# Opening of a two-block transformer kernel: the first modulation computed with its weights stationary, and the first norms and products taken in blocks of features

## Chip, cores and metric

The kernel runs on one core of a Trainium2 chip. The metric is the device time of one execution in microseconds, the median over several executions. Matrix products run on TensorE (PE; its weight loads are listed as PEld), element work on VectorE (DVE), ScalarE (ACT) and GpSimd (POOL); SyncE (SP) issues most transfers.

## What is computed

Two transformer blocks over 256 tokens of width 1024, in fp32. The opening of the first block is what the change touches:

```
c_act = silu(c); c_ctx_act = silu(c_ctx)
shift, scale = (c_act @ w_ada[:, 0:2048] + b_ada[0:2048]) split in two     # for x, and the same for ctx
h     = rmsnorm(x,   g_mix) * (1 + scale)   + shift                        # latent stream
h_ctx = rmsnorm(ctx, g_mix) * (1 + scale_c) + shift_c                      # context stream
dd, k, v = h @ w_in[:, ...]   and the same three from h_ctx
log_a = log_sigmoid(dd @ w_dec_up + b_dec) / 16                            # decays of the linear attention
```

After it come a chunked gated linear attention in both directions, a convolution branch, a merge, a gated feed-forward net, and the second block (feed-forward, two attentions, feed-forward). The factors of modulation are 1024 x 2048 numbers of `w_ada` (8 MB) applied to two vectors only, `c` and `c_ctx`.

## The kernel before, in words

**Precision.** A product of activations and weights is made of three fp32r products, hi*hi, hi*lo, lo*hi. `split` (ACT: L840, DVE: L1833) makes the two parts of a 1 MB weight unit: ACT copies `raw` to `whi`, DVE subtracts to get `wlo`. The units stand in a ring of three. Plain fp32 products (`mm` on fp32 tiles) are recorded as two matmuls each. Every matmul has a weight load of its own.

**Units.** The first block is a list `P1` of units of 256 columns of `w_in`: dd (decay factors), k0, k1, v0 to v3, q0, q1 and so on. Units dd, k and v are made for both streams, latent (tiles A) and context (tiles B). Each engine has its program in a fixed order written by hand; semaphores tie them. For unit `u`, ACT and DVE evacuate unit `u-1`, split unit `u+2`, and then do their part of the attention (`gla_front`, `gla_step`).

**The opening.** SP issues the loads in this order: the three vectors c, two 1 MB blocks of `w_ada`, eleven small vectors, two blocks, ctx, x, four blocks, the units. PE takes `w_ada` as the moving operand: for each of 8 blocks 8 products with a stationary [128, 2] (c and c_ctx), moving 256 columns (L1756 and the loop before it), into rows [2, 512] of four banks. ACT brings the rows to `arow`, PE turns them into columns by 16 small transposes (L1756), DVE adds biases and gain (`columns`, L1853). `norm(n)` on PE (L1323) transposes the normalised ctx (n = 0) and x (n = 1), 16 transposes each; `modulate` (ACT, L882) and `affine`, `low` (DVE, L1881, L1886) apply the factors and split into hi and lo parts. All of `w_ada` has to be multiplied before any factor is used. Then PE makes unit dd by `first_product`, k0 half 0, `gla(U_K, 0)`, that is `decay_products(0)` and `(1)` (16 recorded matmuls over 32 rows, L1371), k0 half 1, and unit k1 with `decay_products(2)`, `(3)` in its middle.

**The decay chain.** From the decay products on, ACT (`log_decays`, `soft_part`, `decays`, L972 to L992) and DVE (`log_decays`, `sums`, `decayed_keys`, L2017 to L2074) work through absolute value, exp, log, prefix sums and exp again. The split of unit 4 (v1) stands on DVE behind the sums of the first pair of passes, that of unit 5 (v2) behind the sums of the second pair. `turn_keys` (L1387) transposes the decayed keys in the middle of v2 and v3.

**GpSimd** forms the inverse roots of the norms, builds constants, and then computes the later modulation blocks (`adapt`, L750 to L759), each behind a 1 MB load of its own; the first of these loads waits for the end of the factors (`as_mm`), the first `adapt` for all hi and lo parts (`hlo_done` 16).

**Later norms.** `shift_and_scale` (L1357), before norms 2 to 5, makes its columns in the other way: stationary a [128, 128] fp32 piece, moving one column of ones, 16 products, recorded as 32.

Of the kernel before, what the change touches and what calls it, by code (L numbers as in the profile page):

```python
# [15 lines left out]
P = 128  # L16
D = 1024
T = 256
# [40 lines left out]
def unit_banks(base, plan):  # L59

    banks, held, before = [], {}, []
    for n, (kind, m) in enumerate(plan):
        if n == 0:
            b = [0, 7] if kind == "dd" else [0]
# [82 lines left out]
def build(nc, a, out):  # L147
    with ExitStack() as ctx:
# [72 lines left out]
        arow = ada_raw[0:2, :, :].rearrange("p a b -> p (a b)")  # L221
# [31 lines left out]

        XN = at3(24, TT, D)
        HF = at3(32, KD, T)
        HF1 = [at3(0, KD, T), at3(8, KD, T)]
# [63 lines left out]
        ada0_mm = sem("ada0_mm")  # L320
        ada0_row = sem("ada0_row")
# [145 lines left out]
        def unit_source(kind, n):  # L467
# [7 lines left out]
            if kind in first:  # L475
                w, c0 = first[kind]
                return cview(w, c0 + UC * n), KD, UC
# [20 lines left out]
        def _(sp):  # L498
# [54 lines left out]
            for j in range(8):  # L553
                if j == 2:

                    for name, r0 in VEC.items():
                        v = a[name]
                        n = math.prod(v.shape) // P
                        src = bass.AP(tensor=v.tensor, offset=0, ap=[[P, n], [1, P]])
                        sp.dma_start(vrows[r0:r0 + n, :], src).then_inc(vec_in, 16)  # L560
                    for name, r0, n in (("b_ada", 0, 48), ("b_ada_2", 48, 72)):
                        src = bass.AP(tensor=a[name].tensor, offset=0, ap=[[P, n], [1, P]])
                        sp.dma_start(brows[r0:r0 + n, :], src).then_inc(vec_in, 16)
                sp.dma_start(ada0[j], a["w_ada"][0].rearrange("(p k) n -> p k n", k=KD)[:, :, UC * j:UC * j + UC])\  # L564
                    .then_inc(start_ada[j], 16)
                if j == 3:
                    sp.dma_start(ctxX, a["ctx"].rearrange(tok, p=P)).then_inc(x_in[0], 16)
                    sp.dma_start(X[:], a["x"].rearrange(tok, p=P)).then_inc(x_in[1], 16)

            for u, (kind, n) in enumerate(P1):  # L570
                load_unit(u, kind, n)
# [34 lines left out]

        def norm_dest(n):
            return (B_hi, B_lo) if n == 0 else (A_hi, A_lo)

        def norm_bank(n, b):  # L610

            return {0: (4, 5, 6, 0), 1: (1, 2, 3, 4), 2: (5, 6, 7, 2), 5: (4, 6, 7, 2)}.get(n, (4, 5, 6, 2))[b]
# [20 lines left out]

        def norm_fp32(n):
            return HF1[n] if n < 2 else HF

# [36 lines left out]
        def _(pool):  # L673
# [93 lines left out]
            norm(0)  # L767
            norm(1)
# [19 lines left out]
            for d in range(2):  # L788
                pool.dma_start(wdec[RANK * d:RANK * d + RANK, d, :], a["w_dec_up"][0, d]).then_inc(dec_in, 16)
            load_ada(0)  # L790
# [38 lines left out]
        def _(act):  # L829
# [52 lines left out]
            def modulate(n):  # L882
                s = 1 if n == 0 else 0
                h, (hi, lo) = norm_fp32(n), norm_dest(n)
                act.wait_ge(as_done, max(1, n))

                def affine(k, o):
                    return run(o[:, k, :], bank[norm_bank(n, k // 2)][:, k % 2 * T:k % 2 * T + T], ACT.Identity,
                               bias=shift[:, s, k:k + 1], scale=scale[:, s, k:k + 1])

                def high(b):
                    if n == 1:
                        act.wait_ge(h_dve, b + 1)
                    else:
                        act.wait_ge(h_done, b + 1)
                    run(hi[:, 2 * b:2 * b + 2, :], h[:, 2 * b:2 * b + 2, :]).then_inc(hhi_done, 1)

                if n == 1:
                    for b in range(4):
                        high(b)  # L900
                    return
                if n == 0:
                    for b in range(4):
                        act.wait_ge(tr_done, b + 1)
                        for k in (2 * b, 2 * b + 1):
                            ins = affine(k, h)
# [1584 lines left out]
```

## Time and profile before

| | us |
|---|---|
| median of 3 runs | 1217.5 |
| lowest, highest | 1215.88, 1219.05 |
| the profiled execution | 1218.4 |
| its span, first to last instruction | 1216.6 |
| PE busy | 1166.5 (96%) |
| DVE busy | 853.4 (70%) |
| ACT busy | 574.0 (47%) |
| POOL busy | 325.1 (27%) |
| mean granted clock of TensorE | 0.976 |

The span is the time from the first to the last instruction of that one execution; its own time is 1.8 us longer. Busy PE time counts matmuls from start to modelled end, so it says nothing of how fast they follow each other: for that, divide the length of a row of the timeline by its count.
### The profile page before, as it was taken

The numbers are of one execution on the slowest core, as the hardware profiler recorded it, in microseconds if no ns is written. First come the engines' busy times: TensorE is split into PE (matmuls) and PEld (weight loads), VectorE is DVE, ScalarE is ACT, GpSimd is POOL, SyncE is SP. The second block draws the span as 40 slices with busy tenths as digits, with TensorE's granted clock in tenths as the row PEclk, the third lists the DMA queues.
The fourth block names the chain that finished last, engine by engine and source line by source line (L and its number), as shares of the span: only waits on it lengthen the run. The fifth ranks groups of instructions, "written<-read, shape, count | busy, mean of one in ns | idle before, by whom it ended". The sixth has DMA issues, their size and how long they took to land.

```text
span 1216.6 us, 18692 instructions
## 1 busy us (share of the span) xinstructions
PE 1166.5 (96%) x7600; PEld 1040.7 (86%) x7600; DVE 853.4 (70%) x935; ACT 574.0 (47%) x734; POOL 325.1 (27%) x219
## 2 busy tenths in 40 slices
PE   6899999999999899999989999999999989999996
PEld 2599988999999888888878888889998989888885
DVE  0478474489577778877778877788766587755676
ACT  1566434354443364444555444445654625544452
POOL 1376573066565200000020000011156663000000
PEclk9899999999999899999989999999999989999999
DMA  9643645365866648777747777755954655656670
GB/s 310 218 139 105 208 144 168 105 217 186 273 232 218 203 169 275 242 254 257 267 147 255 254 252 246 261 161 190 298 181 149 201 186 179 204 177 201 213 258 35
DMA packets 192354, 250.59 MB, mean 206 GB/s; under 512 B 4763, under 2 KB 171870, under 8 KB 192158
## 3 DMA queue, kind: packets, MB, share of 16 engines
q1 hardware_dynamic: 183838, 217.44, 54.9%
q0 software_dynamic: 8448, 32.18, 7.7%
q8 instruction: 50, 0.82, 0.3%
q14 instruction: 18, 0.15, 0.0%
HBM read 248.56 MB, written 1.05 MB: 205 GB/s over the span
## 4 chain that ended last, share of the span: by engine, by line
PE 77%; DVE 13%; ACT 4%; issue 3%; SPq 2%; DMA 1%; POOL 0%; POOLq 0%; DVEq 0%; ACTq 0%
PE twin L1272 74%; DVE arena L1819 4%; DVE wlo L1819 3%; ACT arena L838 2%; DVE arena L1827 2%; SPq L564 1%; DMA raw<-in_w_in 1%; ACT whi L838 1%; PE twin L1340 1%; DVE X L1819 1%; DVE A_both L1819 1%; PE twin L1607 0%; DVE B_lo L1819 0%; DVE X L1827 0%; ACT L838 0%
## 5 line engine op out<-in xcount | busy, mean ns | idle before, releaser
L1272 PE MATMUL twin<-A_both,whi 128*128 128x256 f32 (+1 forms) x2224 | 584.7, 340 | 2.5 <-DVE arena L1819 1.1
L1819 DVE TENSOR_TENSOR wlo<-raw,whi 128x2048 fp32r<-128x2048 f32 x170 | 422.0, 2484 | 158.9 <-ACT whi L838 158.8
L1272 PE MATMUL twin<-A_both,wlo 128*128 128x256 f32 x1640 | 440.1, 281 | 0.0
L838 ACT ACTIVATE whi<-raw 128x2048 fp32r<-128x2048 f32 x170 | 325.1, 1912 | 217.9 <-PE twin L1272 212.1
L1272 PEld LDWEIGHTS twin<-A_both,whi 128*128 128x128 f32 x2224 | 375.1, 191 | 45.9 <-issue 6.7
L1272 PEld LDWEIGHTS twin<-A_both,wlo 128*128 128x128 f32 x1640 | 312.3, 190 | 11.3 <-DVE A_both L1819 0.4
L838 ACT ACTIVATE arena<-twin 128x512 f32<-128x512 f32 (+6 forms) x168 | 88.8, 554 | 125.5 <-PE twin L1272 84.8
L838 ACT ACTIVATE arena<-arena 128x512 f32<-128x512 f32 (+7 forms) x132 | 70.0, 559 | 164.3 <-DVE arena L1819 128.6
L756 POOL TENSOR_TENSOR ada_raw<-ada_raw,arena 128x2048 f32<-128x2048 f32 x24 | 104.7, 4361 | 145.9 <-DMA ada_raw<-in_w_ada 135.0
L1272 PE MATMUL twin<-whi,A_both 128*128 128x256 f32 x640 | 123.9, 295 | 15.4 <-DVE A_both L1819 10.3
L1272 PE MATMUL twin<-whi,B_hi 128*128 128x512 f32 (+2 forms) x340 | 126.8, 373 | 0.2 <-DVE B_lo L1819 0.2
L1272 PE MATMUL twin<-arena 128*2 128x256 f32 (+11 forms) x752 | 115.8, 318 | 11.3 <-DMA arena<-in_w_ada 11.1
L1272 PE MATMUL twin<-wlo,B_hi 128*128 128x512 f32 (+2 forms) x340 | 125.2, 368 | 0.0
L1272 PE MATMUL twin<-whi,B_lo 128*128 128x512 f32 (+2 forms) x340 | 125.2, 368 | 0.0
L1272 PEld LDWEIGHTS twin<-whi,A_both 128*128 128x128 f32 x640 | 105.2, 202 | 17.2 <-DVE A_both L1819 10.7
L1272 PEld LDWEIGHTS twin<-arena 128*128 128x128 f32 (+6 forms) x752 | 79.6, 155 | 39.4 <-issue 15.6
L1819 DVE TENSOR_TENSOR arena<-arena,twin 128x512 f32<-128x512 f32 x92 | 62.3, 684 | 62.4 <-ACT arena L838 49.3
L720 POOL TENSOR_SCALAR arena<-arena 128x1 f32<-128x1 f32 x4 | 1.6, 393 | 375.4 <-ACT arena L838 375.3
L1827 DVE SCALAR_TENSOR_TENSOR arena<-ada_raw,arena 128x256 f32 (+1 forms) x196 | 95.1, 485 | 7.0
L1272 PE MATMUL twin<-wlo,A_both 128*128 128x256 f32 x320 | 93.4, 292 | 0.0
L1272 PEld LDWEIGHTS twin<-whi,B_lo 128*128 128x128 f32 x340 | 64.2, 189 | 11.3 <-issue 0.7
L1272 PEld LDWEIGHTS twin<-wlo,B_hi 128*128 128x128 f32 x340 | 64.2, 189 | 10.7
(128 smaller groups left out, 1203.7 us busy)
## 6 DMA issues: line engine op xcount, KB each, us to landing
raw<-in_w_in SPq DMA_DIRECT2D x49, 1024.0 KB, 5.8
raw<-in_ffn_w_in SPq DMA_DIRECT2D x44, 1024.0 KB, 5.1
ada_raw<-in_w_ada POOLq DMA_DIRECT2D x28, 1024.0 KB, 6.2
ada_raw<-in_w_ada SPq DMA_DIRECT2D x24, 1024.0 KB, 5.4
raw<-in_w_ffn_in SPq DMA_DIRECT2D x22, 1024.0 KB, 5.1
raw<-in_ffn_w_out SPq DMA_DIRECT2D x22, 1024.0 KB, 5.0
raw<-in_w_ffn_out SPq DMA_DIRECT2D x11, 1024.0 KB, 5.1
arena<-in_w_ada SPq DMA_DIRECT2D x8, 1024.0 KB, 11.9
```

The costliest lines, as they stand in the source:

```text
L564: sp.dma_start(ada0[j], a["w_ada"][0].rearrange("(p k) n -> p k n", k=KD)[:, :, UC * j:UC * j + UC])\
L720: link(nc.gpsimd.tensor_scalar(p[0], p[0], EPS, None, ALU.add))
L756: link(nc.gpsimd.tensor_tensor(v[:], v[:], c3[:, :, s:s + 1].to_broadcast([P, KD, UC]), ALU.mult))
L838: return nc.scalar.activation(o, i, f, **kw)
L1272: return nc.tensor.matmul(o, l, r, start=start, stop=stop, **kw)
L1340: ins = nc.tensor.transpose(bank[norm_bank(n, b)][:, c:c + P], src[:, t, P * k:P * k + P], ident)
L1819: return nc.vector.tensor_tensor(o, x, y, op)
L1827: return nc.vector.scalar_tensor_tensor(out=o, in0=x, scalar=sc, in1=y, op0=op0, op1=op1)
```

## The change

The eight blocks of `w_ada` become stationary, in pieces of 128 x 128, and the two vectors move: 128 products of two moving columns in place of 64 of 256. The factors then come out as columns, so that `arow`, its four evacuations and the 16 small transposes are gone. The feature axis is cut in four quarters of 256; each quarter's shift and scale (blocks j = q and j = 4 + q) is used as soon as it is there: DVE makes the factors (`start_columns`), ACT the context and DVE the latent stream (`start_quarter`), PE transposes a quarter (`start_turn`) and adds the quarter's share to the sums of dd (`decay_part`, now 32 stationary columns of weights) and of k0 (`key_part`). The whole of k0 now stands ahead of `gla(U_K, 0)`. Only 128 columns of unit dd are loaded and 32 split. The loads are reordered; on POOL the two norms stand behind the constants, and its first load waits for the last column group. `turn_keys` of the context moves from v2 to v3, that of the latent stream from the first to the second half of v3, their evacuations on ACT by one unit.

```diff
@@ unit_source
+                width = P if kind == "dd" else UC
+                return cview(w, c0 + UC * n, width), KD, width
@@ sync
+            load_start(0)
+            sp.dma_start(ctxX, a["ctx"].rearrange(tok, p=P)).then_inc(x_in[0], 16)
...
+            load_start(4)
+            sp.dma_start(X[:], a["x"].rearrange(tok, p=P)).then_inc(x_in[1], 16)
+            load_start(1)
+            load_unit(0, *P1[0])
+            load_unit(1, *P1[1])
+            for j in (5, 2, 6, 3, 7):
+                load_start(j)
@@ gpsimd
-                    pool.wait_ge(as_mm, 1)
+                    pool.wait_ge(start_cols, 4)
@@ scalar
+            def start_quarter(q):
+                h, ks = start_h[1][q], slice(2 * q, 2 * q + 2)
+                act.wait_ge(start_mod, q + 1)
+                act.wait_ge(tr_done, start_turned(0, q))
+                for m in range(2):
+                    k = 2 * q + m
+                    ins = run(h[:, m, :], bank[norm_bank(0, q)][:, T * m:T * m + T], ACT.Identity,
+                              bias=shift[:, 1, k:k + 1], scale=scale[:, 1, k:k + 1])
+                ins.then_inc(h_done, 1)
+                act.wait_ge(h_done, q + 1)
+                run(B_hi[:, ks, :], h).then_inc(hhi_done, 1)
+                act.wait_ge(h_dve, q + 1)
+                run(A_hi[:, ks, :], start_h[0][q]).then_inc(hhi_done, 1)
@@ scalar: gla_front
-                if u == U_V + 2:
+                if u == U_V + 3:
                     for g in range(4):
                         ctx_key_tokens(g)
-                if u == U_V + 3:
+                if u == U_Q:
                     for g in range(4):
                         key_tokens(g)
@@ scalar: body (vector alike)
-            modulate(0)
-            modulate(1)
+            act.wait_ge(landed[0], 16)
+            run(dd_part(whi[0]), dd_part(raw[0])).then_inc(hi_ready, 1)
+            start_quarter(0)
+            split(1)
+            start_quarter(1)
+            start_quarter(2)
+            split(2)
+            start_quarter(3)
@@ tensor: gla
-                if (u, half) == (U_V + 2, 0):
+                if (u, half) == (U_V + 3, 0):
...
-                if (u, half) == (U_V + 3, 0):
+                if (u, half) == (U_V + 3, 1):
@@ tensor
+            def start_columns(j):
+                x, q = divmod(j, 4)
+                if q and x == 0:
+                    pe.wait_ge(start_mod, q)
+                pe.wait_ge(start_ada[j], 16)
+                for m in range(2):
+                    c = 2 * (KD * x + 2 * q + m)
+                    for k in range(KD):
+                        ins = mm(bank[3][:, c:c + 2], ada0[j][:, k, P * m:P * m + P], c3[:, k, 0:2],
+                                 k == 0, k == KD - 1)
...
+            def decay_part(q):
...
+                for s, x in ((1, B), (0, A)):
+                    pe.wait_ge(hlo_done, 4 * q + (2 if s else 4))
+                    for k in (2 * q, 2 * q + 1):
+                        ins = three(bank[0][0:2 * RANK, T * s:T * s + T], (wh[:, k, :], wl[:, k, :]),
+                                    (x[0][:, k, :], x[1][:, k, :]), True, k == 0 and s == 1, k == KD - 1,
+                                    skip_group_check=True)
+            def key_part(q):
...
+                for x, o in ((B, bank[b[1]]), (A, bank[b[0]])):
+                    for half in range(2):
+                        for k in (2 * q, 2 * q + 1):
+                            ins = step_product(1, o[:, T * half:T * half + T], x, half, False, k,
+                                               k == 0 and half == 0, None, False)
@@ tensor: body
-            for j in range(8):
...
-                for k in range(KD):
-                    ins = mm(bank[j // 2][0:2, UC * (j % 2):UC * (j % 2) + UC], c3[:, k, 0:2], ada0[j][:, k, :],
-                             k == 0, k == KD - 1)
+            start_columns(0)
...
+            start_columns(4)
+            start_turn(0, 0, 1)
+            start_columns(1)
+            start_turn(1, 0, 1)
+            decay_part(0)
+            start_columns(5)
+            key_part(0)
+            start_columns(2)
+            start_turn(0, 2)
+            start_turn(1, 2)
+            decay_part(1)
+            start_columns(6)
+            key_part(1)
+            start_columns(3)
+            start_turn(0, 3)
+            start_turn(1, 3)
+            start_columns(7)
+            decay_part(2)
+            key_part(2)
+            decay_part(3)
+            key_part(3)
+            gla(U_K, 0)
@@ vector
+            def start_columns(q):
...
+                dve.wait_ge(start_cols, q + 1)
+                tt(shift[:, :, k], v[:, 0, :, k], ..., ALU.add)
+                link(tt(scale[:, :, k], v[:, 1, :, k], ..., ALU.add))
+                stt(scale[:, :, k], scale[:, :, k], 1.0, ..., ALU.add, ALU.mult).then_inc(start_mod, 1)
```

## Rows read from the trace of the kernel before

**Rows 1.** The page: busy time of the engines, and the chain's shares by engine

```profile
PE 1166.5 (96%) x7600; PEld 1040.7 (86%) x7600; DVE 853.4 (70%) x935; ACT 574.0 (47%) x734; POOL 325.1 (27%) x219
PE 77%; DVE 13%; ACT 4%; issue 3%; SPq 2%; DMA 1%; POOL 0%; POOLq 0%; DVEq 0%; ACTq 0%
```

**Rows 2.** The chain of waits in order of time: start us, us, what

```profile
31.09 13.66 DMA raw<-in_w_in
...
61.96 8.81 PE twin L1272 x60
...
122.03 7.47 PE twin L1272 x48
```

**Rows 3.** Windows: length, busy us (count) by engine, granted clock, DMA share, GB/s

```profile
9.10:14.10 5.00, 4.98 (x12) 1.52 (x13) 0.00 (x0) 0.00 (x0) 0.00 (x0) 1.00 1.07 316
27.90:31.20 3.30, 3.30 (x8) 0.94 (x9) 1.51 (x2) 3.30 (x8) 2.70 (x5) 0.50 1.10 348
31.30:36.50 5.20, 5.20 (x25) 1.89 (x23) 1.80 (x2) 0.11 (x1) 4.83 (x13) 1.00 1.10 349
118.90:122.00 3.10, 0.03 (x1) 0.00 (x1) 3.10 (x4) 2.33 (x6) 3.02 (x2) 1.00 0.00 0
123.40:126.80 3.40, 3.40 (x18) 3.40 (x17) 3.40 (x9) 3.06 (x4) 1.65 (x2) 0.50 1.00 323
420.30:423.70 3.40, 3.40 (x34) 3.40 (x33) 2.00 (x4) 1.02 (x4) 2.40 (x5) 1.00 0.85 325
423.80:427.10 3.30, 3.30 (x18) 3.30 (x18) 0.97 (x5) 0.80 (x2) 0.38 (x1) 0.50 1.09 379
1017.70:1021.00 3.30, 3.30 (x18) 3.30 (x17) 1.51 (x5) 0.98 (x3) 0.77 (x1) 0.50 1.07 375
```

**Rows 4.** PE in order of time: start us, us, engine, line, operands, count

```profile
9.12 16.45 PE L1272 MATMUL twin<-arena 128*2 128x256 f32 x64 [9.12 <-DMA arena<-in_w_ada]
...
36.50 1.97 PE L1340 MATMUL twin<-arena 128*128 128x128 f32 x16
...
45.40 0.90 PE L1756 MATMUL twin<-arena,ada_raw 2*128 2x2 f32 x12
...
52.04 0.42 PE L1272 MATMUL twin<-B_lo,whi 128*128 128x256 f32 x1
52.26 0.41 PE L1272 MATMUL twin<-B_hi,wlo 128*128 128x256 f32 x1
...
65.05 0.28 PE L1272 MATMUL twin<-B_lo,whi 128*128 128x256 f32 x1
65.17 0.28 PE L1272 MATMUL twin<-B_hi,wlo 128*128 128x256 f32 x1
...
67.90 3.72 PE L1272 MATMUL twin<-arena 32*128 32x256 f32 x16
```

**Rows 5.** PE in order of time, around norm 2

```profile
420.29 3.65 PE L1272 MATMUL twin<-arena 128*128 128x1 f32 x32
423.80 3.58 PE L1340 MATMUL twin<-arena 128*128 128x128 f32 x16
```

**Rows 6.** PEld in order of time: two weight loads with nothing ahead of them

```profile
53.43 0.29 PEld L1272 LDWEIGHTS twin<-B_hi,whi 128*128 128x128 f32 x1 [0.41 <-DVE B_lo L1819]
56.44 0.19 PEld L1272 LDWEIGHTS twin<-B_hi,whi 128*128 128x128 f32 x1 [0.65 <-DVE B_lo L1819]
```

**Rows 7.** DVE and POOL in order of time

```profile
54.80 0.99 DVE L1824 TENSOR_SCALAR arena<-twin,arena 128x256 f32<-128x256 f32 x2
55.71 0.68 DVE L1819 TENSOR_TENSOR B_lo<-arena,B_hi 128x512 fp32r<-128x512 f32 x1
...
81.95 3.93 DVE L1819 TENSOR_TENSOR arena<-arena 128x512 f32<-128x512 f32 x1
...
119.56 2.28 DVE L1819 TENSOR_TENSOR wlo<-raw,whi 128x2048 fp32r<-128x2048 f32 x1
...
244.10 0.30 POOL L683 TENSOR_SCALAR arena<-arena 128x4 f32<-128x4 f32 x1 [45.74 <-ACT arena L838]
```

More of the change, by code:

```diff
@@ L63, in unit_banks @@
         if n == 0:
[L64 removed]
+            b = [0]
         elif kind in DUAL:
@@ L1753, in _ @@
-            for k in range(16):
-                if k % 4 == 0:
-                    pe.wait_ge(ada0_row, k // 4 + 1)
-                ins = nc.tensor.transpose(bank[7][:, 2 * k:2 * k + 2], arow[:, P * k:P * k + P], ident[0:2, 0:2])
-            ins.then_inc(as_mm, 1)
-            norm(1)
+            def start_columns(j):
[8 more added lines that the diff above has]
+                                 k == 0, k == KD - 1)
+                if x:
+                    ins.then_inc(start_cols, 1)
@@ new lines, in start_turn @@
+            def start_turn(n, *quarters):
+                src = norm_source(n)
+                for t in range(TT):
+                    pe.wait_ge(xn_done, 2 * n + t + 1)
+                    for q in quarters:
+                        if q >= 2:
+                            pe.wait_ge((h_done, h_dve)[n], q - 1)
+                        for m in range(2):
+                            k = 2 * q + m
+                            c = T * m + P * t
+                            ins = nc.tensor.transpose(bank[norm_bank(n, q)][:, c:c + P], src[:, t, P * k:P * k + P],
+                                                      ident)
+                        if t == TT - 1:
+                            ins.then_inc(tr_done, 1)
@@ new lines, in start_quarter @@
+            def start_quarter(q):
+                ks = slice(2 * q, 2 * q + 2)
+                start_columns(q)
+                dve.wait_ge(start_mod, q + 1)
+                dve.wait_ge(tr_done, start_turned(1, q))
+                for m in range(2):
+                    k = 2 * q + m
+                    ins = ts(start_h[0][q][:, m, :], bank[norm_bank(1, q)][:, T * m:T * m + T],
+                             scale[:, 0, k:k + 1], shift[:, 0, k:k + 1], ALU.mult, ALU.add)
+                ins.then_inc(h_dve, 1)
+                for s, (hi, lo) in ((1, (B_hi, B_lo)), (0, (A_hi, A_lo))):
+                    dve.wait_ge(hhi_done, 2 * q + (1 if s else 2))
+                    rest(lo[:, ks, :], start_h[s][q], hi[:, ks, :]).then_inc(hlo_done, 2)
@@ L2403, in _ @@
             norm(1)
-            split(0)
-            dve.wait_ge(vec_done, 1)
-            columns(0, 7, VEC["g_mix"], 0, (0, 1))
-            for b in range(4):
-                low(0, b)
-                dve.wait_ge(tr_done, 4 + b + 1)
-                for k in (2 * b, 2 * b + 1):
-                    ins = affine(1, k)
-                ins.then_inc(h_dve, 1)
-            for b in range(4):
-                low(1, b)
+            dve.wait_ge(hi_ready, 1)
+            rest(dd_part(wlo[0]), dd_part(raw[0]), dd_part(whi[0])).then_inc(lo_ready, 1)
+            start_quarter(0)
             split(1)
+            start_quarter(1)
+            start_quarter(2)
+            split(2)
+            start_quarter(3)
             for u in range(N1):
@@ L2421, in _ @@
                 gla_step(2 * (u - 1 - U_Q) + 1)
-                split(u + 2)
+                if u:
+                    split(u + 2)
                 gla_front(u)
```

167 lines of the change are left out of this document (65 added, 102 removed).

## Prediction

> **What bounds the kernel now.** Read the page first: PE is busy 96% of the span, and the chain that ended last runs over PE for 77% of it [rows 1]. From the first complete unit to the end only a shorter use of PE, or an earlier start of it, moves the time. Then the chain of waits of the first 130 us [rows 2]. It runs through the transfers until 44.8 us, through PE's k0 and the decay products (61.96 to 70.8; these begin at 67.90 [rows 4]), then for 51 us through ACT and DVE, and back to PE at 122.03, the first product of unit v2. The windows show why: PE sat idle from 118.9 to 122.0 while DVE was busy throughout [rows 3], and the last thing DVE finished before 122.03 is `wlo` of v2, at 119.56 + 2.28 = 121.84 [rows 7]. So the opening is worth what it does to one moment, the start of the decay products at 67.90: v2 starts 122.03 - 67.90 = 54.1 us later, and from there PE has no long idle time that this stretch could give back.
>
> So I ask: when do the decay products start after the change?
>
> **Prices on PE.** All products of the new opening are weight loads with short or medium streams. I take them at both levels of the clock:
> - A column product (plain fp32, stationary 128 x 128, one moving column): 32 records in 420.29 to 423.80, 0.110 us each, at granted clock 1.00 [rows 3, 5]. Two moving columns change nothing in that, the load sets it. At clock 0.50 there is no such row. An unhindered load of 128 columns took 0.19 us at full clock (56.44) and 0.29 at half (53.43) [rows 6]; the 0.10 between them is the length of the stream at full clock, so at half clock a record costs twice the time, 0.213, as dense ones do. Bounds: 0.110 (if loads overlapped in full) and 0.29 (if not at all); I take 0.213, which every other 128-column record has there.
> - fp32r product, 256 moving: 0.12 (65.05 to 65.17) and 0.213 at half clock (52.04 to 52.26) [rows 4]. The dd product with 32 stationary columns has the same stream; I keep its price.
> - Transpose: 1.97/16 = 0.12 full, 3.58/16, in starts 0.213, half [rows 4, 5].
>
> **Which clock.** This decides it. PE was never idle from 420.29 to 427, and yet behind 3.5 us of column products the clock stood at 0.50 instead of 1.00 (423.8 to 427.1); norm 5 shows the same from 1017.7 on [rows 3, 5]. One such group costs the clock, with no pause anywhere. It came back after 3.4 us of dense records (27.9 to 31.2) or after some 5 (9.1 to 14.1, where 12 records in 5.0 us, against 52 in the 11.4 us behind them, are the half clock) [rows 3, 4]. The new opening starts at half clock, as now, and has eight groups of 32 records, each like the group that lost the clock. I therefore price it at half clock throughout and then give back what the dense pieces between can win.
>
> The Trainium skill, "TensorE: Matmul & The Clock Gate", section "The HAM clock gate", says that the clock falls after the engine has been idle and that activity releases it. By that rule a queue of column products without pauses keeps the full clock; rows 3 and 5 show it falling without one, so the trace does not agree. What the rule would give is rival 1.
>
> **PE's order, in time.**
> - Eight column groups, 32 x 0.213 = 6.8 us each, 54.5. Removed are 128 records of 256 moving, 16.45 us for the first 64 [rows 4], and 16 small transposes.
> - Transposes of vectors 0.5; 32 transposes 6.8; dd 48 x 0.213 = 10.2; k0 96 x 0.213 = 20.4.
> - Waits: the first group starts with its block at about 9.0 (9.12 now). Groups 0 and 4, the vectors and the first turns end at 9.0 + 6.8 + 0.5 + 6.8 + 1.7 = 24.8. Group 1 needs the first factors, and DVE makes them only behind its part of dd. Twelve blocks of 1 MB had landed at 44.75 [rows 2], at 9.0 the first, 3.25 us each; dd is complete with 5.5 of them, at 23.6, its two casts and the factors take 1.5 to 2. I let group 1 start at 25.7. Behind it, quarter 0 of the latent stream (two affines 0.99, then hi, then lo 0.68 [rows 7]) lets PE wait 1.3 us around `decay_part(0)`. Later quarters are turned and modulated while a group runs and nothing waits; nor does data hold PE, for a block arrives every 3.25 us and a group takes 6.8.
> - Sum at half clock: 25.7 + six groups 40.8 + 24 transposes 5.1 + dd 10.2 + k0 20.4 + 1.3 = 103.5.
> - Given back: the last 72 records (decay and key parts 2 and 3) are dense without a break. After some 4.8 us at half clock the rest, 50 records, run at 0.12: 4.6 us less, 98.9.
> - Two `key_part`s of 5.1 us and one stretch of turns and `decay_part(1)` (4.3 us) may each win the clock at their end and carry it into the next group, which then runs about 3.4 us at full clock before it falls, as at 420.3: 3.3 us back each. Between none and three of them (0 to 9.9) I take 7.6, a little over two. The decay products start at 91.3 (89 to 99), against 67.90: 23.4 later.
>
> All of k0 now lies ahead of them. Its second half stood behind them before, under the chain of DVE; after the change this cover is gone, and PE has less to do while DVE works: 3.6 (the products) + 5.8 x 2 (k1) + 3.6 + 4 x 5.8 (v0, v1) and some 3 for half clock make 45 from the start of the decay products to the end of v1, so it waits 9 us for `wlo` of v2 where it waited 3.1. That is why I carry the whole 23.4 and not 23.4 less k0's half. After so long a pause PE comes back at half clock and stays there somewhat longer than now (0.50 from 123.4 to 126.8 [rows 3]): +1. The chain of 54.1 has its own bounds. Some of its DVE steps ran beside `adapt` on POOL at several times their length (3.93 at 81.95 against 0.68 for the same size [rows 7]), and POOL's start moves with the last group, about 4 us later against the chain; if all collisions went, PE's own 45 would be the bound, 9 less; 3 more if they fall worse.
>
> **Edits at nothing.** The four evacuations of `arow` and the smaller split of dd free ACT and DVE, which wait for PE here. The constants stand ahead of the norms on POOL: about 6 us of work that starts below 2 us, and the norms are first wanted near 17. SP's queue only changes order; the loads of units 2 and 3 land by 45 to 50, far ahead of their use. POOL's first load now waits for the last column group, near 81, and its first `adapt` shifts by some 28 us, 4 more than PE; it later waits 45.7 us for ACT [rows 7], which covers that. `turn_keys` and its evacuations move behind the chain together; v3 and q0 give them 5.8 us each, so no gain and no loss. If ACT were late there, q0 would wait at most the 2 us of four copies.
>
> **Sum.** 23.4 + 1 = 24.4. The profiled execution is 1218.4, so it would be 1243; against the median, 1217.5 (0.9 below), I say **1242 us**. With the bounds above (21 to 32 for the opening, -9 to +3 for the chain) this case reaches from 1230 to 1252.
>
> **Rivals.**
> 1. The clock stays at its full level. Mixed with dense parts, the groups might not cost it. For: each group behind dense work ran its first 3.4 us at 1.00 [rows 3]. Against: what followed both of them. From group 1 on: 25.7 + 6 x 3.5 + 24 x 0.12 + dd 5.8 + k0 11.5 + 1.3 = 68.2. The decay products start 0.3 us later than now, and what was saved, k0's half, goes into PE's wait for DVE. No change: 1218, between 1215 and 1221. Chance 0.07.
> 2. Column records cost 0.11 at either clock. The Trainium skill, same page, "LDWEIGHTS (loading the stationary operand)", gives a load as P / 1.2 ns, the same at both levels; by it the eight groups would take an estimated 27 us and the trace, 0.19 against 0.29 [rows 6], speaks against it. From rows alone, with 0.110 per record and the rest as in my sum: 25.7 + 21 + 5.1 + 10.2 + 20.4 + 1.3 - 4.6 = 79, some 2 less for the clock won between: 77, 9 later than now, 1227. Chance 0.06.
> 3. Faster: two moving columns ride on loads that follow each other as at 45.40, 0.07 us [rows 4], at full clock. A group takes 2.2 us, less than its block's transfer, and the transfers are the bound: the last block is complete with 11.5 blocks where the twelfth landed at 44.75, so 43.1; group 7, the decay and key parts 2 and 3: 43.1 + 2.2 + 72 x 0.12 = 54. 14 earlier, 1204. Against: those were loads of 2 rows in transposes; the one-column products of rows 5 did not follow so closely. With any smaller gain from a chain that meets less of POOL, chance 0.09.
>
> **Chances.** Forecast 0.78, all of it slower; rival 2 adds 0.06: slower by over 0.3% (3.7 us, about what a measurement of this kernel tells from none) 0.84. Within 0.3%: 0.07. Faster: 0.09. The range of 8 in 10 reaches down to rival 2: 1226 to 1252.
>
> **What would show it.** Granted clock 0.50 in most of the windows between 9 and 90 us; column groups of 32 records lasting 6 to 7 us; the decay products (32 rows, 16 records) near 91; PE idle some 9 us before v2; from v2 on the same picture as now, shifted. The prediction is wrong if the column groups last 3.5 us, if the clock is 1.00 between 30 and 80, or if v2 starts much less than 54 us behind the decay products.

## The result, and the profile after

The changed kernel takes **1239.78 us** (median of 4 runs, 1238.14 to 1243.09), the kernel before, on the same chip, 1218.28 (1215.88 to 1220.97). The ratio is 1.0163, 95% interval 1.013 to 1.0195: slower, by some 21.5 us. Forecast were 1242, between 1226 and 1252. The profiled execution after took 1240.74, its span is 1239.0.

The page of the changed kernel, first its busy times, then the chain's shares by engine (they answer to [rows 1]):

```profile
PE 1188.5 (96%) x7712; PEld 1082.9 (87%) x7712; DVE 857.2 (69%) x941; ACT 571.0 (46%) x729; POOL 313.1 (25%) x219
...
PE 80%; DVE 11%; ACT 4%; issue 3%; DMA 1%; POOL 0%; SPq 0%; POOLq 0%; DVEq 0%; ACTq 0%
```

PE's share is the same 96% in a span 22.4 us longer: busy time does not tell good work from slow work. The queue of SP, 2% of the chain before, is gone from it: behind the first block the transfers no longer set the pace of the opening. PE does.

PE of the changed kernel in order of time (start us, us, engine, line, operands, count). A column group is the 32 records of one block of `w_ada`. The rows are the eight column groups and what stands between some of them, then the decay products and the first products of v1 and v2 (they answer to [rows 4]):

```profile
10.01 6.96 PE L1272 MATMUL twin<-arena 128*128 128x2 f32 x32 [10.01 <-DMA arena<-in_w_ada]
...
17.26 6.99 PE L1272 MATMUL twin<-arena 128*128 128x2 f32 x32
24.11 1.95 PE L1754 MATMUL twin<-arena 128*128 128x128 f32 x8
25.89 6.99 PE L1272 MATMUL twin<-arena 128*128 128x2 f32 x32
...
36.11 0.39 PE L1272 MATMUL twin<-B_hi,whi 128*32 128x256 f32 x1 [1.43 <-DVE B_lo L1873]
...
38.65 6.82 PE L1272 MATMUL twin<-arena 128*128 128x2 f32 x32
...
50.60 3.79 PE L1272 MATMUL twin<-arena 128*128 128x2 f32 x32
...
58.17 4.07 PE L1272 MATMUL twin<-arena 128*128 128x2 f32 x32
...
67.37 3.94 PE L1272 MATMUL twin<-arena 128*128 128x2 f32 x32
...
72.69 6.83 PE L1272 MATMUL twin<-arena 128*128 128x2 f32 x32
...
90.51 3.72 PE L1272 MATMUL twin<-arena 32*128 32x256 f32 x16
...
128.03 0.77 PE L1272 MATMUL twin<-whi,A_both 128*128 128x256 f32 x2 [6.75 <-ACT arena L849]
...
145.20 0.47 PE L1272 MATMUL twin<-whi,A_both 128*128 128x256 f32 x2 [3.30 <-ACT arena L849]
```

Read the lengths: five groups of 6.8 to 7.0 us and three of 3.8 to 4.1, for the same 32 records (a row's length also holds the last record's own 0.25 to 0.36 us). The windows say why (stretch, length, busy us (count) by engine PE, PEld, DVE, ACT, POOL, then granted clock, DMA share, GB/s):

```profile
38.60:45.50 6.90, 6.90 (x35) 6.90 (x34) 1.56 (x1) 0.00 (x0) 0.00 (x0) 1.00 1.10 348
50.60:54.30 3.70, 3.70 (x34) 3.70 (x34) 0.00 (x0) 0.00 (x0) 0.00 (x0) 1.00 0.04 13
58.20:62.30 4.10, 4.10 (x35) 4.10 (x34) 0.02 (x1) 0.00 (x0) 0.00 (x0) 0.86 0.00 0
62.30:67.40 5.10, 5.10 (x25) 5.10 (x26) 3.28 (x8) 3.98 (x5) 0.00 (x0) 0.50 0.00 0
72.70:79.60 6.90, 6.90 (x35) 6.86 (x35) 0.04 (x1) 0.00 (x0) 0.00 (x0) 0.50 0.20 72
79.60:85.00 5.40, 5.40 (x27) 4.97 (x26) 2.65 (x7) 2.17 (x4) 0.99 (x1) 0.50 0.54 193
90.50:94.20 3.70, 3.70 (x18) 2.93 (x17) 3.70 (x2) 2.48 (x6) 3.62 (x2) 1.00 0.00 0
125.00:128.00 3.00, 0.00 (x0) 0.00 (x0) 2.50 (x2) 3.00 (x7) 2.64 (x3) 0.67 0.00 0
```

The last group ran at 0.50 throughout, the one of 50.60 at 1.00. The first of these rows is the trap that the table of times warned of: the column shows 1.00 where no change had been seen yet, but 35 records in 6.90 us are the half clock. DMA stands at 0.04 in the window of the group of 50.60 and at 0.00 from 58.2 to 67.4: all blocks had landed, and PE was still at work on them.

Behind v2 nothing is new. From v2 to norm 2 it takes 442.65 - 145.20 = 297.45 us (298.26 before), and from norm 2 to the end 796.3 (796.3 before). The first products of norm 2 answer to [rows 5], where they start at 420.29 (the view read here ends at 445, inside the row, so it counts 22 of the 32):

```profile
442.65 2.52 PE L1272 MATMUL twin<-arena 128*128 128x1 f32 x22
```

All of the 22.4 us of span lies ahead of v2, which starts 145.20 - 122.03 = 23.2 later; 0.8 of that is won back by norm 2.

### The profile page after: what moved, and what is told of

It reads as the page before. It is cut to its first block, busy times and chain, and to the rows that moved or that the text cites. A ratio compares the mean times of both kernels' runs of the same rounds, so it can differ in the third digit from the quotient of the medians.

```text
span 1239.0 us, 18934 instructions
## 1 busy us (share of the span) xinstructions
PE 1188.5 (96%) x7712; PEld 1082.9 (87%) x7712; DVE 857.2 (69%) x941; ACT 571.0 (46%) x729; POOL 313.1 (25%) x219
## 4 chain that ended last, share of the span: by engine, by line
PE 80%; DVE 11%; ACT 4%; issue 3%; DMA 1%; POOL 0%; SPq 0%; POOLq 0%; DVEq 0%; ACTq 0%
PE twin L1272 78%; DVE arena L1873 3%; DVE wlo L1873 3%; ACT arena L849 2%; DVE arena L1881 2%; ACT whi L849 1%; PE twin L1333 1%; DVE X L1873 1%; DMA arena<-in_w_ada 1%; PE twin L1754 1%; DVE arena L2129 0%; DVE arena L2131 0%; PE twin L1599 0%; DVE X L1881 0%; DVE arena L2415 0%
## 5 line engine op out<-in xcount | busy, mean ns | idle before, releaser
L1272 PE MATMUL twin<-A_both,whi 128*128 128x256 f32 (+2 forms) x2224 | 586.0, 340 | 1.1 <-DVE arena L1873 1.1
L1873 DVE TENSOR_TENSOR wlo<-raw,whi 128x2048 fp32r<-128x2048 f32 (+1 forms) x170 | 430.1, 2531 | 154.1 <-ACT whi L849 153.8
L1272 PE MATMUL twin<-A_both,wlo 128*128 128x256 f32 (+1 forms) x1640 | 440.1, 281 | 0.0
L849 ACT ACTIVATE whi<-raw 128x2048 fp32r<-128x2048 f32 (+1 forms) x170 | 323.6, 1904 | 210.6 <-PE twin L1272 208.0
L1272 PEld LDWEIGHTS twin<-A_both,whi 128*128 128x128 f32 (+1 forms) x2224 | 375.6, 191 | 44.4 <-issue 6.4
L1272 PEld LDWEIGHTS twin<-A_both,wlo 128*128 128x128 f32 (+1 forms) x1640 | 312.0, 190 | 11.2
L849 ACT ACTIVATE arena<-twin 128x512 f32<-128x512 f32 (+5 forms) x167 | 88.8, 557 | 122.0 <-PE twin L1272 93.3
L1272 PE MATMUL twin<-arena 128*128 128x2 f32 (+9 forms) x880 | 132.3, 306 | 10.0 <-DMA arena<-in_w_ada 10.0
L1272 PEld LDWEIGHTS twin<-arena 128*128 128x128 f32 (+5 forms) x880 | 117.3, 206 | 18.8 <-issue 10.0
L1272 PEld LDWEIGHTS twin<-whi,A_both 128*128 128x128 f32 x640 | 105.4, 202 | 22.6 <-issue 14.0
L768 POOL TENSOR_TENSOR ada_raw<-ada_raw 128x1024 f32<-128x1024 f32 x24 | 75.8, 3159 | 1.9
```

What stands on the lines that cost most here:

```text
L768: link(nc.gpsimd.tensor_tensor(v[:, 0:4, :], v[:, 0:4, :], v[:, 4:8, :], ALU.add))
L849: return nc.scalar.activation(o, i, f, **kw)
L1272: return nc.tensor.matmul(o, l, r, start=start, stop=stop, **kw)
L1873: return nc.vector.tensor_tensor(o, x, y, op)
```

## The experiments

Four quantities tell the runs apart. They are the starts, in us, of the first decay products, of v2 and of norm 2 in the profiled execution, and PE's waits from the first of these to the start of v2. Times are medians; each kernel was measured together with the kernel before, and the ratio is to those runs, so it is the ratio, not the time, that compares two rows.

| | decay products | waits | v2 | norm 2 | time | ratio, 95% interval |
|---|---|---|---|---|---|---|
| before | 67.90 | 3.1 | 122.03 | 420.29 | 1218.28 | |
| after | 90.51 | 6.7, 3.3 | 145.20 | 442.65 | 1239.78 | 1.0163, 1.013 to 1.0195 |
| e3_cols | 84.35 | 2.8 | 138.17 | 435.53 | 1236.18 | 1.0149, 1.0097 to 1.0201 |
| e9_k0_first | 73.73 | 6.4, 2.3 | 130.12 | 439.25 | 1236.55 | 1.0115, 1.0076 to 1.0153 |
| e1_fill1 | 81.57 | 3.9, 2.9 | 136.34 | 433.67 | 1232.02 | 1.0110, 1.0055 to 1.0165 |
| e2_fill2 | 94.10 | 4.0, 2.6 | 148.74 | 443.37 | 1242.12 | 1.0190, 1.0136 to 1.0243 |
| e7_burst | 73.84 | 7.0, 1.3 | 126.62 | 419.25 | 1220.85 | 1.0016, 0.9985 to 1.0046 |
| e5_pool_held | 89.55 | none | 136.16 | 430.43 | 1228.21 | 1.0068, 1.0044 to 1.0093 |
| e10_turns_back | 90.73 | 6.8, 3.1 | 145.31 | 442.58 | 1245.63 | 1.0192, 1.015 to 1.0234 |
| e4_decay_first | 61.50 | none | 116.61 | 427.03 | 1221.14 | 1.0003, 0.9975 to 1.0032 |
| e6_decay_first_turns | 60.81 | none | 120.51 | 417.52 | 1215.41 | 0.9966, 0.9935 to 0.9997 |
| e11_first_held | 61.59 | none | 116.72 | 415.77 | 1214.10 | 0.9954, 0.9931 to 0.9976 |
| e8_all | 70.63 | none | 121.48 | 424.45 | 1220.57 | 0.9999, 0.9968 to 1.0031 |

The interval of e1 overlaps that of the changed kernel, and so do those of e2, e3 and e10: for these four the starts in the trace carry the argument, not the time.

**1. The clock: a dense product between the column products.** In the changed kernel:

```diff
@@ start_columns, behind each column product but the last of eight
+                        mm(bank[3][0:2, 256:512], dense[:, 0:2], dense, False, True, ...)   # twice in e2_fill2
```

`dense` is 256 columns of ones that ACT makes at the start; the result is not used.

> The changed kernel with one dense product (fp32r, 2 stationary columns, 256 moving, into unused columns of the same bank, result unused) behind each of the column products except the last of a group of eight; nothing else. Theory, the clock: the column products cost what they do because they lose TensorE's full clock. Filled, the clock stays at 1.00 from some 15 us on, a group of columns takes 3.5 to 4.5 us instead of 6.9, the decay products start at 69 to 76 us instead of 90.5, and the time is 1219 to 1226, 14 to 21 less than the changed kernel. Rival, the load: the loads of 128 columns are slow by themselves and the clock is a symptom; then the fill only adds 0.11 to 0.21 us per product: groups of 8.5 us or more, decay products at 100 or later, time above 1250.

Measured: 1232.02, 7.8 below the changed kernel (the two ratios overlap), and the decay products at 81.57 instead of 90.51. Not the 1219 to 1226, and not the 69 to 76, that I expected; the rival's 1250 and more fell too. PE of this kernel in windows, columns as above; the second is one group, from its first product on:

```profile
26.50:33.00 6.50, 6.50 (x44) 6.50 (x43) 0.00 (x0) 1.65 (x3) 0.00 (x0) 1.00 1.10 349
51.00:54.70 3.70, 3.70 (x45) 3.70 (x45) 0.00 (x0) 0.00 (x0) 0.00 (x0) 1.00 0.00 1
54.70:62.00 7.30, 7.30 (x77) 7.19 (x76) 0.61 (x4) 0.22 (x1) 0.00 (x0) 1.00 0.01 2
62.00:81.50 19.50, 19.50 (x191) 19.18 (x190) 7.33 (x13) 8.32 (x11) 3.07 (x2) 1.00 0.34 108
```

From 49.7 on the clock is at 1.00 and stays there through four column groups, to 94.0: the fill holds it. In the changed kernel it fell three times in that stretch. But the first four groups ran at half clock (44 records in 6.5 us; 6.98, 6.86, 6.85 and 6.85 us from the first record's start to the last's): the fill did not raise it. At half clock a group of 46 records took 6.85 where one of 32 took 6.60, so 14 products more cost 0.25 us; at full clock it took 3.83 against 3.54 for the group that ran at 1.00.

> As the one before with two dense products behind each column product. Theory, the clock: full clock as well, but a group now takes 5 to 6 us, because the second stream can't hide behind a load: decay products at 79 to 84, time 1228 to 1234, so worse than one fill and still better than none. If one fill is too little to hold the clock, this one shows it: then it is the faster of the two. Rival, the load: 14 us or more slower than with one fill, above 1264.

Measured: 1242.12, groups of 9.9 us at half and 5.42 at full clock: the second product is paid for in full, and one is enough to hold the clock. The group of 5 to 6 us is as expected, the decay products (94.10 for 79 to 84) and the time (1228 to 1234) are not, for here too the first groups ran at half clock; the rival fell, as the second product costs 10 us and not 14.

**2. The clock again: bursts that raise it.** On top of one fill:

```diff
@@ tensor: body
+            burst(32)                 # 32 products of dense, ahead of the first group
             start_columns(0)
@@
             start_turn(0, 0, 1)
+            burst(16)
             start_columns(1)
```

`burst(n)` is n products of `dense`; their results are not used either.

> The kernel with one dense product behind each column product (the first experiment), and two bursts of such products that nothing uses: 32 while PE waits for the first block, 16 behind the first transposes. Theory, the clock: there the fill held the full clock but did not bring it back; it came at 49.7 only. Raised before group 0, it stays: all groups near 3.8 us, the decay products at 69 to 73 instead of 81.6, time 1219 to 1224. Rival: the clock falls in the groups all the same, or the bursts cost what they win: 1230 to 1236.

Measured: 1220.85, as expected; 19 below the changed kernel (18 by the ratios), no longer told from the kernel before. The windows of this kernel show the full clock from 10.2 on in all of the opening but 17.0 to 27.2:

```profile
10.20:17.00 6.80, 5.73 (x62) 5.23 (x61) 0.00 (x0) 1.27 (x4) 0.00 (x0) 1.00 0.95 317
17.00:27.20 10.20, 10.20 (x62) 9.43 (x62) 3.74 (x8) 5.45 (x12) 3.90 (x8) 0.50 1.11 344
27.30:73.00 45.70, 44.07 (x447) 42.99 (x446) 14.93 (x27) 12.70 (x17) 2.31 (x2) 1.00 0.68 215
```

The decay products start at 73.84. So of the 22.6 us that they were late, 16.7 went with the clock, the cost of the fill included, and v2 came 18.6 earlier. This is the main cause of the slowdown, shown by taking it away. The 5.9 us that are left are as long as k0's second half, 5.8. (At 17.0 the clock fell behind a wait of 1.1 us for a block, in spite of the fill.)

Not all of the 19 us is the opening, though. From v2 to norm 2 this execution takes 292.63 us, 4.8 less than the changed kernel and 5.6 less than the kernel before, at a granted clock of 1.00 where the changed kernel has 0.98. Whether the edit or this one execution did that is not shown.

**3. The form of the modulation alone.** The kernel before, with its modulation in the new form and nothing else:

```diff
@@ tensor: body, blocks j = 0 to 7 in their old order
-                    ins = mm(bank[j // 2][0:2, ...], c3[:, k, 0:2], ada0[j][:, k, :], k == 0, k == KD - 1)
+                for m in range(2):
+                    for k in range(KD):
+                        ins = mm(bank[7][:, c:c + 2], ada0[j][:, k, P * m:P * m + P], c3[:, k, 0:2], ...)
```

> The kernel before with one part of the change alone: the modulation by 128 stationary weight pieces and two moving columns, straight into columns (no rows, no evacuation, no small transposes); order of loads, norms, dd, k0 and all else as before. Theory: the form of the product is the whole loss. Eight groups without dense work between, 6.8 us each, end near 9.1 + 54.5 + 4 = 68 where the factors' products ended at 47.6: the decay products start 18 to 22 us later than 67.9, time 1236 to 1240. Rival, the order: if the loss came from the new order by quarters (more waits, k0 ahead of the decay products), this kernel stays at 1217 to 1221.

Measured: 1236.18, just inside the 1236 to 1240 expected; the rival, the order, would have left the kernel at 1217 to 1221. PE of this kernel in order of time:

```profile
8.90 27.43 PE L1266 MATMUL twin<-arena 128*128 128x2 f32 x128 [8.90 <-DMA arena<-in_w_ada]
...
36.55 13.67 PE L1266 MATMUL twin<-arena 128*128 128x2 f32 x64
...
53.53 10.55 PE L1266 MATMUL twin<-arena 128*128 128x2 f32 x64
```

256 records without a wait for a block, 0.21 us each in the first two rows; the last row holds one stretch at full clock (53.8 to 57.2), which the expectation of 18 to 22 us left out. The decay products come 16.4 us later, v2 16.1. Taking the opening by quarters seems to have bought nothing of this back: in the changed kernel they come another 6.2 later, and k0's second half, which stands there ahead of them, is 5.8 long.

**4. k0 ahead of the decay products, alone.**

```diff
@@ tensor: gla, kernel before
-                if (u, half) == (U_K, 0):
+                if (u, half) == (U_K, 1):
                     decay_products(0)
                     decay_products(1)
```

> The kernel before with one edit: decay_products(0) and (1) stand behind both halves of k0, where they stood between them. The second half is 48 records at 0.12 us, 5.8. Theory (k0's second half was cover under the decay chain, and v2 hangs on the start of the decay products): the decay products start at 73.7 instead of 67.9, v2 some 54 us behind them near 128, PE waits about 9 before v1 and v2 together where it waited 3.1, and the time is 5 to 6 us above the kernel before, 1223 to 1225; this is also what the changed kernel's remainder of 5.8 between it and the run with the modulation alone in the new form should be. Rival (PE's own work sets the time here and the order does not matter): within 1 us of the kernel before, PE's waits unchanged. Rival 2 (the chain only moves partly, since DVE meets less of GpSimd's work when it starts later): +1 to +3.

Measured: 1236.55, far more than the 1223 to 1225 expected, and more than either rival gave. The decay products start 5.83 us later, as expected. PE has the same 7600 matmuls as before and the time is still 1.15% longer, so the first rival, PE's own work, falls. The rest is new waits: 6.4 us before v1, 2.3 before v2, 5.6 before `turn_keys`. PE, then DVE and GpSimd of this kernel, in order of time:

```profile
130.12 0.47 PE L1272 MATMUL twin<-whi,A_both 128*128 128x256 f32 x2 [2.31 <-ACT arena L838]
141.74 3.68 PE L1393 MATMUL twin<-arena 128*128 128x128 f32 x16 [5.64 <-DVE arena L1819]
```

```profile
100.55 2.25 DVE L2063 COPY arena<-arena 128x2 f32<-128x2 f32 x1
...
119.17 2.26 DVE L2063 COPY arena<-arena 128x2 f32<-128x2 f32 x1
...
131.71 3.61 DVE L2074 COPY arena<-arena 128x2 f32<-128x2 f32 x1
```

```profile
100.03 2.74 POOL L757 TENSOR_TENSOR ada_raw<-ada_raw 128x1024 f32<-128x1024 f32 x1
...
118.66 2.73 POOL L757 TENSOR_TENSOR ada_raw<-ada_raw 128x1024 f32<-128x1024 f32 x1
...
130.73 4.57 POOL L756 TENSOR_TENSOR ada_raw<-ada_raw,arena 128x2048 f32<-128x2048 f32 x1 [5.18 <-DMA ada_raw<-in_w_ada]
```

A copy of two columns, 0.17 us by itself (127.48), takes 2.25: it ends at 102.80, GpSimd's operation at 102.77. So do the other two, at 121.43 and 121.39, and at 135.32 and 135.30. Each of the three came 0.5 to 1.0 us after the start of an operation on GpSimd and stood until that one's end. Here the decayed keys (L2074) were hit three times and are done 68.0 us behind the decay products (60.1 in the changed kernel), and `turn_keys` waits 5.6 us for them; the clock stands at 0.50 from 139.3 to 146.1. The shift by 5.8 thus costs 8.1 at v2 and 19 at norm 2. How much a delay costs depends on where it lets the two engines meet.

The Trainium skill, "SBUF — State Buffer", section "SBUF: two separate sides", says that DVE and GpSimd share one pair of ports: a DVE operation that reads two inputs in SBUF or runs in a mode of two ports, and a GpSimd operation, exclude each other, and the one that starts first has the pair for its whole length. These ends, within 0.04 us, agree; in which mode the copies ran, no run here shows.

**5. GpSimd out of the way.** The changed kernel with GpSimd's modulation blocks from the second on held until v2 is split (one of the eight blocks moves behind the roots of the outputs):

```diff
@@ gpsimd
-            for n in range(8):
+            for n in range(7):
+                if n == 1:
+                    pool.wait_ge(lo_ready, 6)
                 adapt(n)
```

> The changed kernel; POOL computes its first later modulation block as before and holds the next ones back until v2's weights are split (7 instead of 8 of them ahead of the head norms, 9 instead of 8 behind). Theory: behind the decay products the time is set by the chain on ACT and DVE, and this chain is lengthened by what runs on POOL beside it (DVE steps of 4.5 us instead of 1.2, 2.7 instead of 0.7). Held back, PE's waits of 6.7 us (ahead of v1) and 3.2 us (ahead of v2) nearly go, with the half clock behind them: 10 to 14 us less than the changed kernel, 1226 to 1230. Rival: the chain is as long as it is by its own instructions and POOL's are only beside it: 1238 to 1241, both waits as they were.

Measured: 1228.21, 11.6 below the changed kernel, the two intervals apart; confirmed. PE has no wait at v1 or v2, and v2 starts 46.6 us behind the decay products, where it was 54.7: PE's own work. In the changed kernel DVE was caught like this (DVE, then GpSimd, in order of time). The scan of 103.30 ends 1.08 us behind the first GpSimd operation, the subtraction of 107.86 0.54 us behind the second:

```profile
103.30 4.53 DVE L2129 TENSOR_TENSOR_SCAN arena<-arena 128x512 f32<-128x512 f32 x1
107.86 2.71 DVE L1873 TENSOR_TENSOR arena<-arena 128x512 f32<-128x512 f32 x1
```

```profile
103.09 3.66 POOL L767 TENSOR_TENSOR ada_raw<-ada_raw,arena 128x2048 f32<-128x2048 f32 x1 [5.83 <-DMA ada_raw<-in_w_ada]
106.83 3.20 POOL L768 TENSOR_TENSOR ada_raw<-ada_raw 128x1024 f32<-128x1024 f32 x1
```

In the run with the blocks held, the same scan takes

```profile
107.09 1.23 DVE L2131 TENSOR_TENSOR_SCAN arena<-arena 128x512 f32<-128x512 f32 x1
```

**6. The turns back in their old places**, in the changed kernel (`turn_keys` and its evacuations where the kernel before has them):

> The changed kernel with turn_keys and its evacuations in their old places (context in the middle of v2, latent in the first half of v3). The prediction put this edit at nothing. Here DVE is through with the decayed keys at 150.6 and PE would come to the context's turn at about 152.5, so no wait: within 1 us of the changed kernel, norm 2 within 1 us of 442.7. Rival (the late chain meets this step too, as it did when the decay products alone were moved ahead in the kernel before): a new wait of 2 to 5 us before the turn, and 2 to 5 us more in the time.

Measured: norm 2 at 442.58 and no wait at the turn. The median, 1245.63 (1238.21 to 1247.66, 6 runs), lies 5.9 above the 1239.78 of the changed kernel, where "within 1 us" was expected, and the profiled execution, 1242.15, 1.4 above the profiled one after. The trace bears the theory out and shows none of the rival's waits; the time doesn't confirm it, and the ratios (1.0192 and 1.0163, the intervals overlap) are too wide to settle a few us.

**7. Decay products earlier, in the kernel before**, right behind unit dd:

```diff
@@ tensor
+                    decay_products(0)      # behind first_product of dd
+                    decay_products(1)
@@ gla
-                if (u, half) == (U_K, 0):
-                    decay_products(0)
-                    decay_products(1)
```

> The kernel before with the decay products (0) and (1) right behind dd, ahead of both halves of k0. Theory: the time hangs on the start of the decay products and, behind it, on the longer of PE's own work and the chain on ACT and DVE. They start 5.5 to 6 us earlier, PE's idle time of 3.1 us before v2 and most of the 0.9 us before k0 go: 3 to 4 us less than before, 1213.5 to 1215.5. Rival: the chain on ACT and DVE slips back by what else these engines must do there (splits of units 2 and 3), and nothing is gained: 1217 to 1219.

Measured: 1221.14, ratio 1.0003, no gain: expectation missed, the rival's result, though not by the rival's path, the splits. v2 has no wait and starts 5.4 earlier, but the turn of the context's keys now waits for DVE, which met GpSimd in the decayed keys (its L756 ran from 116.14 for 3.91 us); a second wait of 2.8 us follows at 174.7, and in the profiled execution (1225.2) norm 2 comes 6.7 later than before:

```profile
115.89 4.71 DVE L1818 TENSOR_TENSOR arena<-arena 128x512 f32<-128x512 f32 x2
120.52 2.36 DVE L2073 COPY arena<-arena 128x2 f32<-128x2 f32 x1
```

```profile
127.66 3.67 PE L1393 MATMUL twin<-arena 128*128 128x128 f32 x16 [5.13 <-DVE arena L1818]
```

The next run adds the change's own later turns:

> The kernel with the decay products ahead of k0 (the fourth experiment), and the transposes of decayed keys one unit later, as in the changed kernel. Theory: there the gain ahead of v2 went into a wait of 5.1 us for the decayed keys, that is, the chain is met a second time; moved back, that wait is gone: 1213 to 1216, 2 to 5 us less than the kernel before. Rival: the chain is met a third time (the states and scores from q1 on, 3.6 us of waits near 175 in that trace), and nothing is left: 1217 to 1220.

Measured: 1215.41, as expected, without that wait; ratio 0.9966 (0.9935 to 0.9997), just clear of the kernel before, but not of e4, whose interval overlaps it. Ahead of v2 the programs of e4 and e6 are the same, and yet v2 starts 55.1 us behind the decay products in the one and 59.7 in the other, with PE busy throughout in both. The granted clock tells them apart: in this stretch it was 0.97 in e4 and 0.89 in e6, which stood at 0.50 from 63.8 to 70.6 and from 87.8 to 94.5. Starts of single executions can thus differ by some 4 us without any edit.

The last adds the hold of GpSimd's blocks:

> The kernel before with the decay products right behind dd, the turns one unit later (as in the run of that name, 1215.4) and GpSimd's modulation blocks from the second on held back until v2 is split. Theory (PE had no wait left between the decay products and the later units in that run, so a shorter chain has nothing to give): 1213 to 1217, norm 2 within 1.5 us of 417.5. Rival (GpSimd's work beside DVE still costs the path something): 3 to 6 us less, 1209 to 1212. Rival 2 (holding the blocks makes the modulation of norm 2 late): norm 2 later than 419 and a time over 1218.

Measured: **1214.10** (1212.76 to 1218.52, 12 runs), ratio 0.9954 (0.9931 to 0.9976): faster than both kernels, by 0.5% than the one before. It lies in the theory's 1213 to 1217; norm 2, at 415.77, came 1.75 earlier than in e6, a little outside what I gave. Which of the three edits (earlier decay products, later turns, held blocks) the gain belongs to is not shown: the intervals of e6 and e11 overlap as well.

**8. All of it in the changed kernel**: fill, bursts, GpSimd held, and the decay products behind `decay_part(3)`, ahead of the key parts 2 and 3.

> The kernel of the bursts, with the decay products right behind the last decay part (ahead of key parts 2 and 3), and POOL held back as in the fifth experiment. Theory: decay products at 62 to 66, no collisions of DVE with POOL behind them, so that PE's own work binds up to v2, which starts at 111 to 116 (122 before, 145 after): 1206 to 1214, less than both kernels. Rival: the chain's later meetings (decayed keys, states) take it back, as in the fourth experiment: 1215 to 1221.

Measured: 1220.57, missed, inside the rival's range. The decay products start at 70.63, not at 62 to 66. The 73.84 of e7 less the 48 records of the key parts 2 and 3 (5.8) would be 68.0, so the range was too early by itself; the rest is waits: without the key parts ahead of it, `decay_part(3)` waits 1.6 us for the hi and lo parts of the last quarter, and the decay products 0.8 for ACT. PE of this kernel:

```profile
68.26 0.30 PE L1277 MATMUL twin<-B_hi,whi 128*32 128x256 f32 x1 [1.56 <-DVE B_lo L1890]
```

v2 then starts 50.9 behind the decay products with no wait between: PE's own work, the two key parts included, is the bound there. One new wait of 3.8 us for DVE follows at 172.4.

## Why the prediction was right, and where not in detail

- **The question asked was the right one.** v2 starts 54.7 us behind the decay products (54.1 before), and behind v2 the kernel is the old one. By terms, between the profiled executions: the decay products 22.6 later (23.4 forecast), the chain 0.6 longer (carried unchanged), the stretch behind v2 0.8 shorter (1 longer forecast). That is 22.4 for 24.4.
- **The clock.** The prediction priced the groups at half clock. From the first record's start to the last's the eight groups measured 6.60, 6.64, 6.63, 6.47, 3.54, 3.72, 3.69 and 6.47 us. That the groups themselves cost the clock is shown by e1: the last four, with one dense product between every two column products, kept it.
- **The price** of a record at half clock, 0.213, was right (6.60/31 = 0.213). What carried it is that every other record with 128 stationary columns costs that at half clock; the working from the two lone loads, 0.29 less 0.19, is no argument for it. Rival 2 fell, its 0.11 at half clock; rivals 1 and 3 with it.
- **Given back.** The prediction took "a little over two" of the three groups behind dense pieces; it was all three, at the places named (50.60, 58.17, 67.37), 2.9 to 3.1 us each, 8.8 for the 7.6 put in. The decay products came at 90.51 for 91.3, v2 at 145.20 for 145.4.
- **Some of that closeness is luck.** The first group started at 10.01 and not at 9.0; the 0.9 us that PE was to wait for the first factors did not occur, so group 1 began at 25.89 for 25.7 all the same. And the term of +1 behind v2 didn't come. More so the picture "from v2 on the same as now, shifted": a shift of 5.8 us alone made 8.1 at v2 and 19 at norm 2 in e9, and from v2 to norm 2 the runs took from 292.6 (e7) to 310.4 us (e4). That 54.1 and 298.26 hardly moved in the changed kernel could not be known from the rows of before; the bounds of -9 to +3 were given for the first alone.
- **The waits** were 10.0 for 9, but in two parts. 6.7 of it stands before v1: there k1 has to be evacuated by ACT, behind the exponentials of the second pair of passes. The prediction had only `wlo` of v2 in view. Even at v2 it read the wait a little wrongly: the chain of waits goes over ACT's evacuation of v0, which ended at 121.88, 0.04 later than `wlo`; in the changed kernel they end at 145.06 and 145.00. The sum was the same, for all of them hang on the same sums of DVE. The first row is from the chain of waits, the second from DVE in order of time, both of the changed kernel:

```profile
143.47 1.59 ACT arena L849 x3
```

```profile
142.72 2.28 DVE L1873 TENSOR_TENSOR wlo<-raw,whi 128x2048 fp32r<-128x2048 f32 x1
```

- **Bounds of the chain.** "9 less if all collisions went" measured 8.1 less at v2 (e5), and 11.6 in the time. In runs where PE waited for the chain, v2 came 52.8 (e7) to 56.4 us (e9) behind the decay products.
- **k0's second half as cover.** Carried in full, 5.8, and the 6.2 between e3 and the changed kernel agree. But e9 shows that its worth is not a fixed sum: alone in the kernel before it cost 18.6 between the profiled executions, 14 by the ratio.
- **Edits at nothing.** The turns were tested, and no wait came of them (e10). The others (constants ahead of the norms, order of loads, the smaller split) were not run by themselves; the sum leaves them little. That later turns bring "no gain and no loss" may not hold in general: with the decay products early, the wait of 5.1 us at the turn is there with the old turns (e4) and gone with the later ones (e6).

## What to carry to other kernels

Turning a product around so that the weights stand and two vectors move saves columns and pays in weight loads; in this kernel such groups also cost TensorE its full clock, and most of what lay between them ran at half. Price them at half clock, or put one wide product, wanted or not, between every two, and something dense ahead to raise the clock. Even so the new form only drew level with the old one (e7, ratio 1.0016). Where DVE holds the chain, look at what GpSimd does at the same moments before moving anything: in the changed kernel, holding GpSimd's work back was worth 12 us.

## What the runs showed of the hardware that was not expected

- A product of 256 columns between column products held the full clock for 44 us (49.7 to 94.0), yet column groups so filled did not raise it in the 39 us before. It rose within stretches of products of 256 columns: in `key_part(0)` at 49.7, or in a burst of 32 (at 10.2 in e7).
- At half clock such a product rode along at almost no cost: 0.25 us for 14 of them in a group.
- A DVE copy of 128 x 2, 0.17 us alone, took 2.25, 2.26 and 3.61 us behind the start of a GpSimd operation and ended with it within 0.04 us (e9).
- The same program ahead of v2 took 55.1 us in one execution and 59.7 in another, at mean granted clocks of 0.97 and 0.89 (e4, e6).

**Open.** Which property of the column groups costs the clock was not separated. The times of one kernel varied by up to 1.2% between executions (e6, 1210.81 to 1225.63); how much of that is the clock, as between e4 and e6, and how much the meetings of DVE and GpSimd was not followed, as only one execution of each has a trace.
